# Weight splits ahead of the norms, a transposed input, and latent attention's entry in another order

## What is computed

```python
def rms_norm(x, g):
    return x * lax.rsqrt(jnp.mean(x * x, axis=-1, keepdims=True) + NORM_EPS) * g

for i in range(DEPTH):                    # pool, conv, latent attention, pool
    x = x + mixer(rms_norm(x, norm[i]), ...)
# pool mixer:   u, z = split(xn @ w_in); pooled means of u; per-group matmul; * silu(z); @ w_out
# latent attention:
h = xn @ w_in                             # q_lat 384, kv_lat 256, k_rope 64, z 2048
q  = rms_norm(q_lat, q_norm) @ w_q_up     # 16 heads x (128 + 64 rotary)
kv = rms_norm(kv_lat, kv_norm) @ w_kv_up  # 16 heads x (128 keys + 128 values)
o  = causal_block_attention(q_nope, rope(q_rope), k_nope, rope(k_rope), v)
x  = x + (o * silu(z)) @ w_out
# second block, twice: attention, then
h = rmsnorm(x, mlp_norm); x = x + square(relu(h @ w_ff1)) @ w_ff2
```

## Time and profile before

| what | value |
|---|---|
| median of 3 runs | 2774.82 us (2774.36 to 2774.85) |
| the profiled execution | 2773.87 us |
| its span, first to last instruction | 2772.1 us |
| busy: PE, DVE, ACT, POOL | 98%, 56%, 42%, 22% of the span |
| mean granted PE clock | 0.993 |
| moved from memory | 234.6 MB, 85 GB/s over the span |

### The profile page before, as it was taken

One profiled execution on the slowest core, in us unless ns is written; L12 is line 12 of the kernel. 1 busy time (PEld: TensorE's weight loads), 2 busy tenths in 40 slices (PEclk: granted clock), 3 DMA queues, 4 the chain that ended last, 5 costly groups with the idle time before them and its releaser, 6 DMA issues.

```text
span 2772.1 us, 32060 instructions
## 1 busy us (share of the span) xinstructions
PE 2708.0 (98%) x12950; PEld 2264.8 (82%) x12950; DVE 1563.4 (56%) x2322; ACT 1151.1 (42%) x1849; POOL 618.2 (22%) x402
## 2 busy tenths in 40 slices
PE   7999999999989999999999999999999999999998
PEld 5888888888868888878888888778888888778886
DVE  6557555344465646556565768744435668744433
ACT  4323322222345636533235777522224667522223
POOL 1000111111125625400003651411102451411100
PEclk9999999999999999999999999999999999999999
DMA  3322323332321222222232221223333211223332
GB/s 125 103 92 91 110 88 103 99 99 91 99 60 60 65 85 63 84 92 95 95 99 94 77 71 37 76 91 99 94 97 101 76 65 43 76 86 97 93 102 71
DMA packets 68836, 238.78 MB, mean 86 GB/s; under 512 B 7632, under 2 KB 10192, under 8 KB 68688
## 3 DMA queue, kind: packets, MB, share of 16 engines
q1 hardware_dynamic: 68688, 236.73, 26.9%
HBM read 234.60 MB, written 2.10 MB: 85 GB/s over the span
## 4 chain that ended last, share of the span: by engine, by line
PE 90%; DVE 5%; ACT 2%; POOL 1%; issue 1%; DMA 0%; SPq 0%; DVEq 0%; POOLq 0%; ACTq 0%
PE ps L409 29%; PE ps L410 29%; PE ps L411 29%; POOL acc L2252 1%; PE ps L497 1%; PE ps L711 1%; PE ps L710 1%; DVE xl L1502 1%; PE ps L435 1%; DVE ptl L1498 0%; DVE yl L1498 0%; DVE g L1498 0%; PE ps L558 0%; PE ps L557 0%; DVE x L1524 0%
## 5 line engine op out<-in xcount | busy, mean ns | idle before, releaser
L409 PE MATMUL ps<-xh,wh 128*128 128x512 f32 x1936 | 766.3, 396 | 25.1 <-DVE wl L1490 16.3
L410 PE MATMUL ps<-xl,wh 128*128 128x512 f32 x1936 | 757.4, 391 | 0.0
L411 PE MATMUL ps<-xh,wl 128*128 128x512 f32 x1936 | 757.3, 391 | 0.0
L895 ACT ACTIVATE wh<-raw 128x1024 fp32r<-128x1024 f32 (+2 forms) x453 | 464.1, 1026 | 582.0 <-PE ps L411 581.4
L1490 DVE TENSOR_TENSOR wl<-raw,wh 128x1024 fp32r<-128x1024 f32 (+1 forms) x339 | 417.7, 1233 | 141.2 <-ACT wh L895 141.2
L409 PEld LDWEIGHTS ps<-xh,wh 128*128 128x128 f32 x1936 | 366.1, 189 | 107.3 <-DVE wl L1490 23.8
L410 PEld LDWEIGHTS ps<-xl,wh 128*128 128x128 f32 x1936 | 366.4, 189 | 77.3 <-issue 2.6
L411 PEld LDWEIGHTS ps<-xh,wl 128*128 128x128 f32 x1936 | 365.7, 189 | 77.1
L409 PE MATMUL ps<-yh,wh 128*128 128x512 f32 x1088 | 424.9, 391 | 2.2 <-DVE wl L1490 1.5
L410 PE MATMUL ps<-yl,wh 128*128 128x512 f32 x1088 | 423.4, 389 | 0.0
L411 PE MATMUL ps<-yh,wl 128*128 128x512 f32 x1088 | 423.4, 389 | 0.0
(11 more groups left out here) (259 smaller groups left out, 3585.6 us busy)
## 6 DMA issues: line engine op xcount, KB each, us to landing
raw<-in_ff SPq DMA_DIRECT2D x120, 512.0 KB, 3.6
raw<-in_pool_in SPq DMA_DIRECT2D x64, 512.0 KB, 3.3
raw<-in_conv_in SPq DMA_DIRECT2D x64, 512.0 KB, 3.3
raw<-in_pool_out SPq DMA_DIRECT2D x32, 512.0 KB, 3.3
raw<-in_qk SPq DMA_DIRECT2D x32, 512.0 KB, 3.6
raw<-in_pool_grp SPq DMA_DIRECT2D x16, 512.0 KB, 3.3
raw<-in_conv_out SPq DMA_DIRECT2D x16, 512.0 KB, 3.4
raw<-in_mla_z SPq DMA_DIRECT2D x16, 512.0 KB, 3.5
```

The costliest lines, as they stand in the source:

```text
L409: pe.do.matmul(o, lh, rh_, start=start, stop=False)
L410: pe.do.matmul(o, lh, rl_, start=False, stop=False)
L411: return pe.do.matmul(o, ll, rh_, start=False, stop=stop)
L895: act.do.activation(h[:, 0:ncol], r[:, 0:ncol], ACT.Copy).then_inc(*mark("whi", ("whi", k)))
```

## The change

There are three parts.

**Splits ahead.** In the first group of each pool layer, and in the first quarter of each MLP, unit i asks for the split of unit i + AHEAD[i]: 6, 7, 8 and 8 for i = 0 to 3, on ACT and DVE. For the later units, and all later quarters of the MLP, it is i + 3. On DVE the pool layer's call stands behind the first addition of the means, the MLP's between the scaling (now the counterpart of L2177) and the low part. Latent attention's first unit asks for unit + 3 ahead of the root.

**Start.** The host passes x transposed as eight blocks of 128x512. SP loads vec, x0, unit 0, x1, unit 1, x2 to x7, then const, unit 2 and strict. The 32 transposes and 32 copies are gone. PE does u0 and u1 together: first all 32 products with x's high parts, then the 16 with the low parts, and the sum of squares comes behind u2 instead of u0. (first_pair was there already for the MLP.)

**Latent attention's entry.** The key and value latents come first (lat3, lat4, kr), then lat0 to lat2. The key and value products of head 0 fill the time before the q latent's norm. The units mz0, mz1, the keys of heads 0 and 1, and the values now stand ahead of scores(0); behind scores(0) only the q products of head 1 are left. The loop begins with head 1. k_high(1) waits for the last scores of head 0, since the two heads share the tile kh.

```diff
+AHEAD = (6, 6, 6, 5, 3)
...
-    for i in range(5):
+    for i in (3, 4):
         add(("lat", i), D["mla_lat"][:, i * 1024:(i + 1) * 1024], 1024)
     add(("kr",), D["mla_lat"][:, 5120:5632], 512, True)
+    for i in range(3):
+        add(("lat", i), D["mla_lat"][:, i * 1024:(i + 1) * 1024], 1024)
     low(True)
+    add(("ke", 0), D["mla_ke"][0], 256)
+    add(("vk", 0), D["mla_vk"][0], 768)
+    add(("mz", 0), D["mla_z"][0, 0], 1024)
     add(("qe", 0), D["mla_qe"][0], 768)
-    add(("mz", 0), D["mla_z"][0, 0], 1024)
-    add(("ke", 0), D["mla_ke"][0], 256)
-    for h in range(15):
+    add(("mz", 1), D["mla_z"][0, 1], 1024)
+    add(("qo", 0), D["mla_qo"][0], 384)
+    for h in range(1, 15):
         if h % 2:
...
+            def first_pair(st, keys, rows):
+                ns = [unit[key] for key in keys]
+                ws = [unit_ready(n) for n in ns]
+                bs = [bank(*key) for key in keys]
+                for k in rows:
+                    pe.wait_ge(*at("xh", st, k))
+                    cc = slice(k * 128, k * 128 + 128)
+                    for (wh, wl), b in zip(ws, bs):
+                        pe.do.matmul(b[:, :], wh[:, cc], XH[k][:, :], start=k == rows[0], stop=False)
+                        pe.do.matmul(b[:, :], wl[:, cc], XH[k][:, :], start=False, stop=False)
+                for key, n, (wh, wl), b in zip(keys, ns, ws, bs):
+                    for k in rows:
+                        pe.wait_ge(*at("xl", st, k))
+                        cc = slice(k * 128, k * 128 + 128)
+                        mm = pe.do.matmul(b[:, :], wh[:, cc], XL[k][:, :], start=False, stop=k == rows[-1])
+                    mm.then_inc(*mark("group", ("mm",) + key, ("wfree", n)))
 
             def pool_layer(j, st):
                 for g in range(4):
-                    for i in range(4):
+                    if j == 0 and g == 0:
+                        first_pair(0, [("u", 0, 0, 0), ("u", 0, 0, 1)], range(8))
+                    for i in range(2 if j == 0 and g == 0 else 0, 4):
                         xgemm(st, "u", j, g, i, first=g == 0 and i == 0)
-                        if g == 0 and i == 0:
+                        if g == 0 and i == (0 if j else 2):
...
+                xgemm(2, "lat", 3, first=True)
+                sum_squares(2)
+                xgemm(2, "lat", 4)
                 xgemm(2, "kr")
+                xgemm(2, "lat", 0)
                 sum_squares("kv")
+                xgemm(2, "lat", 1)
+                xgemm(2, "lat", 2)
+                pe.wait_ge(*at("ll", "kv", 1))
+                k_up(0, unit["ke", 0], 0)
+                v_pair(0, range(1))
+                sum_squares("q")
+                v_pair(0, range(1, 2))
+                xgemm(2, "mz", 0)
+                k_up(1, unit["vk", 0], 512)
                 rope_up(0)
                 q_up(("qn", 0), unit["qe", 0], (0, 256, 512))
+                xgemm(2, "mz", 1)
+                scores(0)
+                q_up(("qn", 1), unit["qo", 0], (0, 128, 256))
...
             def load():
+                act.wait_ge(*at("vec"))
                 for m in range(8):
+                    act.wait_ge(*at("xin", m))
                     act.do.activation(XH[m][:, :], x[m][:, :], ACT.Copy, scale=vcol("pool_norm0", m)).then_inc(
                         *mark("act", ("xh", 0, m)))
+                    if m < 2:
+                        weights(m)
+                for m in range(4):
+                    square(0, m, x[m][:, :], ("xin", m))
+                weights(2)
+                for m in range(4, 8):
+                    square(0, m, x[m][:, :], ("xin", m))
 
             def out_proj(name, rb, done=None, first=0):
                 for m in range(first, 8):
...
-                        weights(unit["u", j, g, i] + 3)
+                        weights(unit["u", j, g, i] + AHEAD[i if g == 0 else 4])
...
                 def k_high(h):
+                    if h == 1:
+                        act.wait_ge(*at("mm", "sc", 0, 34))
...
+                weights(unit["lat", 3] + 3)
+                root(2, 1024)
+                square("kv", 0, KVF[0], ("lat", "kv", 0))
+                taking("lat", 4)
+                square("kv", 1, KVF[1], ("lat", "kv", 1))
                 taking("kr")
                 swap("m", None, "kr", temp("kr"), ("kr",))
+                taking("lat", 0)
                 root("kv", 256)
+                square("q", 0, QF[0], ("lat", "q", 0))
                 latent_high("kv", 2, KVH, KVF)
                 act.wait_ge(*at("t1", "m", "kr"))
                 high(KRH[:, :], temp("t1", "m", "kr"), ("t1", "m", "kr"), ("rqh", "kr"))
+                taking("lat", 1)
+                square("q", 1, QF[1], ("lat", "q", 1))
+                taking("lat", 2)
+                square("q", 2, QF[2], ("lat", "q", 2))
                 taking("ke", 0)
                 k_high(0)
+                taking("vk", 0)
+                root("q", 384)
+                latent_high("q", 3, QH, QF)
+                v_high(0)
+                taking("mz", 0)
+                taking("qe", 0)
+                swap("m", None, 0, ps("qr", 0), ("mm", "qr", 0))
+                q_high(0)
+                taking("mz", 1)
+                rope_high(0)
+                taking("qo", 0)
+                k_high(1)
+                q_high(1)
+                scores(0)
+                silu(0)
...
+                        weights(unit["f1", l, qd, i] + AHEAD[min(i, 4) if qd == 0 else 4])
...
             def load():
+                weights(1)
+                dve.wait_ge(*at("vec"))
+                for m in range(8):
+                    x_low(0, m)
+                weights(2)
...
+                taking("ke", 0)
+                k_low(0)
+                taking("vk", 0)
+                latent("q", 3, QH, QLO, QF)
+                v_low(0)
+                taking("mz", 0)
+                gate(0)
                 taking("qe", 0)
                 turned_cos(0)
                 q_low(0)
+                turned_sum(0)
+                taking("mz", 1)
                 rope_low(0)
+                gate(1)
+                taking("qo", 0)
+                scores(0)
+                k_low(1)
+                q_low(1)
+                sums(0)
...
+            sp.do.dma_start(vec[:, :], D["vec"]).then_inc(*mark("vec", ("vec",), by=16))
+            for m in range(8):
+                sp.do.dma_start(x[m][:, :], D["x"][m]).then_inc(*mark(f"xin{m}", ("xin", m), by=16))
+                if m < 2:
+                    weights(m)
             sp.do.dma_start(const[:, :], D["const"]).then_inc(*mark("consts", by=16))
+            weights(2)
...
-    d["x"] = i["x"][0]
+    d["x"] = np.ascontiguousarray(i["x"][0].T).reshape(8, 128, S)
```

197 lines of the change are left out of this document (64 added, 133 removed).

## The result

The changed kernel took 2753.24 us (median of 4 runs, 2746.51 to 2755.00), the kernel before 2774.84 beside it: a ratio of 0.9916, with a 95% interval from 0.9899 to 0.9934. The forecast was 2737.5, its range ended at 2747. One of the four executions, at 2746.51, was inside the range; the median was not. So 21.6 us were gained where 37.3 were forecast. The profiled execution is that of 2755.00 us, with a span of 2753.2 us; the profiled gain is 18.9.

A forecast was written before the change was run, and what follows sets the result against it. PE, busy 98% of the span, was the bound, leaving its idle time and slow stretches to win back. Gains 7.6 + 7.0 + 2.2 + 3.1 + 11.4 + 6.0 = 37.3 us, from the median 2774.82, gave 2737.5; range 2727 to 2747.

The forecast's parts named there:

- then five rows at 3.1: 1828.4: First MLP: the last five rows take 3.1 us each, ending at 1828.4; PE waits 0.5 and 2.3, gain 2.2.
- the chain comes back as the bound: MLPs: the serial row chain (DVE, POOL, ACT, DVE), 3.1 us, limits f2's first unit; gains only 2.2 and 3.1.
- I take these short new waits to leave the clock alone: MLPs, f2's first unit: new waits of 0.5 and 2.3 us in the first cause no clock fall.
- Rival 2: Short new waits lower the clock at MLPs (1.6, 2.6) and head 1 (about 2), longer slow start (1.5): 2745; chance 20%.
- All else keeps its order: Rest of the kernel, attention layers included: order stays as before; nothing added to the sum.
- Pool layers: Pool layers' first groups: waits for unit 6's low part and slow stretches behind them go; gains 7.6 and 7.0 us.
- Start: Kernel start: PE begins at 10.9 instead of waiting for the third unit; gain 11.4 us, ends 9 and 13.5.
- Rival 3: Start: unit 1 lands with all of the input at 13.5, PE starts 4.9 later: 2742.5; chance 10%.
- Latent attention: Latent attention's entry: turn(0) comes 6.0 us earlier (ends 3 and 8), with waits of 2.0 and 2.1.
- The drain: Latent attention: 1.38 us per table load by the skill page; turn(0) would come 1.4 later; left out of the sum.
- rival 4: Latent attention: head 1's lag stays, each of 14 heads waits 4.1 us again, 57 more: 2795; chance 2%.

The follow-up runs named there:

- e3: Changed kernel, but DVE splits units 9 and 10 of the MLP only behind the eighth row of the first quarter; 2741.50 us, ratio 0.9888.
- e4: Changed kernel, but in the MLP's first quarter DVE scales row i+1 ahead of row i's low part, unit 10 split behind the rows; 2734.77 us.
- e9: Changed kernel with 6 and 13 unused PE products in the MLP's waits for rows 6 and 7; 2745.19 us, ratio 0.9897.
- after: The changed kernel itself, against the kernel before; median 2753.24 us, its profiled execution 2755.00 us.
- e1: The changed kernel once more, unaltered; 2752.45 us, ratio 0.9921.
- e2: Changed kernel with its earlier splits taken out of the two MLPs alone; 2746.04 us, ratio 0.9899.
- e8: Kernel e4, but each attention layer's last differential head's sum of squares stands behind the last stick-breaking head's scores; 2732.42 us, ratio 0.9853.
- e11: Changed kernel with unused products in the waits of e9, the last differential head, the second scores and the first turned probabilities; 2742.98 us.
- e12: Kernel e8 once more, unaltered; 2729.59 us, ratio 0.9848.

## Why the prediction was wrong

The sum put 37.3 us on the gain and the profiled execution had 18.9. Of the 18.4 missing, about 12.8 are the granted clock behind short waits (4.0 in the MLPs, 7.3 in the attention layers, about 1.5 in latent attention), for which the sum held nothing, and 3.4 are rows that were priced too short. The steps one by one:

**MLPs: the step "then five rows at 3.1: 1828.4".** The last two of these five rows hold a split each (units 9 and 10, by the same table AHEAD that the term is about), and a split beside POOL's square adds 0.91 us. The waits were 1.47 + 3.04 = 4.5 instead of 0.5 + 2.3 = 2.8. e3 took the two splits out and had 2.7. The mechanism (the chain comes back as the bound) was right and e4 proved it with 13.2 us; the term was mis-sized by 1.7 in each MLP. With the 2.0 of the next step this makes 7.4 of the 8.3 us missing there; 0.9 stays unassigned.

**MLPs and latent attention: the step "I take these short new waits to leave the clock alone".** Wrong for the pair of 1.47 and 3.04 us in four cases of four, and it cost 2 us in each MLP (e9). For the 2.3 us wait in latent attention it was wrong in 5 of 8 executions. From the first turned probabilities to the second pool layer's norm it is 347.0 to 347.3 us where a slow stretch lies there (after, e1, e4, e9) and 345.8 where none does (e2, e3, e8, e11, e12), against 345.5 before: the stretch costs 1.2 to 1.5 of the 1.75 us. Had the waits been the 2.3 us of the prediction in the MLPs, it would have been right in one layer and wrong in the other (2.14 us, e3). Rival 2 had this mechanism, with 1.6 and 2.6 in the MLPs, and a fifth of the chance.

**Attention layers: the step "All else keeps its order".** The order and the waits did keep, the time did not: 3.1 us behind each 1.35 us wait and 0.5 to 0.6 behind the 1.28 us wait ahead of L728. The prediction read the price of a short wait from a single execution in which these waits had none, and took that for a property of the wait. This was in no rival. Without its 7.3 us the profiled execution would have taken 2747.7, still 0.7 above the range, so it took the MLPs' miss as well. Rival 2's 2745, without the 1.5 that it put on the start, and with 3.4 for the rows and 7.3 for the attention layers, makes 2754.

**Pool layers: right.** 7.25 for 7.0 in the second; together with the start 18.2 for 19.0 in the first; alone 13.2 by the medians, 15.1 in the trace.

**Start: right in size, 0.8 too high with the first pool layer.** PE began at 11.41 and not 10.9. The first 13 products took 5.7 us (up to 17.09), where 11 at double time (5.0) were forecast. The sum of the high products is 20.7 and not 20.5 (10.9 + 5.0 + 4.8). All of this is within what one kernel shows: in the other profiles with the new start PE began at 10.7 to 11.4 and had 9 to 14 slow products, and the first sum of squares came at 29.4 to 30.4, in after at 30.6. Rival 3 (unit 1 lands with all of the input) fell: ACT began to split unit 1 at 8.99, as it landed.

**Latent attention: right up to its own end.** 5.5 of 6.0 at the first turned probabilities, waits of 1.73 and 2.31 for 2.0 and 2.1. The drain that the Trainium skill, ScalarE: Activation LUTs (What ACT_TABLE_LOAD costs), adds to each load would have put the wait at 3.5; it was 2.31, and in the trace the load at 819.27 takes 1.28 us and the exponentials begin 0.01 behind it. The lag of rival 4 did not appear: PE has no further wait in the loop over the heads.

## What to carry to other kernels

When a wait goes from a serial chain of engines, price the chain with everything the same change puts into it, and ask of each instruction moved what runs beside it: a split on DVE cost nothing beside ACT (its 128x512 high parts take 0.63 us with a split beside them and without, after) and 0.9 us beside POOL. In this kernel a wait of TensorE of 3 us or more was worth its length and 2 us on top; one of 1.3 to 2.3 us has an uncertain price that a single profile doesn't show, so the range must hold it, for the waits that the change leaves alone too. Overlap the steps of two rows before splitting further ahead, and take short waits out for the steadiness of the time as well.

## What the runs showed of the hardware

**A wait's price on the clock is a matter of the execution.** In the 14 profiles the waits of PE from 1.27 us on were counted, behind the first 30 us of the program, and each stretch at 0.50 was put to the last such wait that had begun when it began. None was left over:

| wait, us | waits | followed by 1.2 GHz |
|---|---|---|
| 1.27 to 1.41 | 49 | 20 |
| 1.47 to 1.97 | 32 | 2 |
| 2.14 to 2.80 | 11 | 6 |
| 3.04 to 5.22 | 23 | 22 |

The last row is less sure than it looks for the four waits of 3.04 us: their stretches begin 0.4 to 0.65 us into the wait, 1.4 to 1.6 behind the end of the wait of 1.47 us ahead of it, and the stretches behind the waits of 1.28 and 1.35 us begin 1.7 to 2.7 us behind their ends. Without these four the row is 18 of 19. Length isn't all: the wait of 1.55 us at the end of latent attention was followed by none in 14 executions, the shorter ones of 1.28 us (with one of 0.66 us close behind it) and 1.35 us in the attention layers by 20 in 48. A stretch costs 0.5 to 3 us, or nothing where the next wait swallows it (e12). What decides it in a given execution stays open; e4's two layers and e3's two MLPs show that it is neither the instructions nor the wait. The Trainium skill, TensorE: Matmul & The Clock Gate (Part 1: The HAM clock gate), says of the slow products at a kernel's start that their number changes from run to run. The runs agree (9 to 14 slow products at the new start, over eleven profiles), and here the same holds in mid-kernel. It calls the penalty small; against the span it is (some 12 us of 2755 in the profile of after), against a change of 20 us it is not.

**Of DVE's split and POOL's square, the later is held up.** A square of 128x512 takes 1.04 us alone and 1.95 when a 128x1024 subtraction of two inputs began 0.16 us ahead of it (after), and 1.04 again without (e3). The other way round, in 48 pairs of after where the split begins 0.31 us behind the square, the square keeps its 1.04 and the split takes 1.81 us instead of 1.22.

**The granted clock does not show the slow start.** From 11.97 to 17.09 us of after a product began every 0.43 us, where later ones begin every 0.23, while the column says 1.00. The trace of after holds no record of the clock ahead of 17.35 us, and the column reads 1.00 where there is none.
